# The compression's weight blocks take ring slots among the second group's last tiles

## The reference, cut to what matters

```python
def compress_blocks(t, pe, w1, w2):            # t: 256 tokens x 2 key heads x 128
    n_cmp = (s - CMP_BLOCK) // CMP_STRIDE + 1  # 15 blocks of 32 tokens, 16 apart
    idx = np.arange(n_cmp)[:, None] * CMP_STRIDE + np.arange(CMP_BLOCK)[None, :]
    blk = jnp.swapaxes(t[:, idx], 2, 3) + pe
    blk = blk.reshape(b, n_cmp, hk, CMP_BLOCK * d)
    return jax.nn.gelu(blk @ w1) @ w2          # w1: 4096 x 128
```

## Time and profile before

| | |
|---|---|
| median of 3 runs | 2350.07 us (2349.14 to 2352.84) |
| the profiled execution | 2346.51 us, span 2344.7 us |
| PE, DVE, ACT busy | 99%, 63%, 55% of the span |
| mean granted clock of PE | 0.996 |

### The profile page before, as it was taken

The page is one execution under the profiler, slowest core; times in us unless marked ns, Lnnn a source line. Parts: engine busy times, 40 slices in busy tenths (PEclk is TensorE's granted clock), DMA queues, the critical chain, the costliest instruction groups (busy, mean ns, idle before and its releaser), DMA issues.

```text
span 2344.7 us, 32539 instructions
## 1 busy us (share of the span) xinstructions
PE 2310.0 (99%) x12150; PEld 1951.4 (83%) x12150; DVE 1468.5 (63%) x2547; ACT 1299.5 (55%) x2374; POOL 18.3 (1%) x38
## 2 busy tenths in 40 slices
PE   8999999999999999999999999999999999999998
PEld 8877888788888888877888888888888888888886
DVE  5554565665665666876777666756566566665554
ACT  5644555665655545764556546546555555554444
POOL 1000000000000000000000000000000000000000
PEclk9999999999999999999999999999999999999999
DMA  7555565575445565656453326556666666665554
GB/s 230 171 163 151 171 206 189 153 189 171 127 145 195 154 182 174 188 168 177 141 170 111 107 81 234 198 187 177 191 189 189 189 189 189 189 207 190 192 189 165
DMA packets 239596, 409.07 MB, mean 174 GB/s; under 512 B 21504, under 2 KB 54576, under 8 KB 239056
## 3 DMA queue, kind: packets, MB, share of 16 engines
q1 hardware_dynamic: 235424, 393.07, 55.4%
q0 software_dynamic: 3152, 10.57, 1.2%
q10 hardware_dynamic: 864, 3.35, 0.4%
HBM read 400.65 MB, written 6.29 MB: 174 GB/s over the span
## 4 chain that ended last, share of the span: by engine, by line
PE 94%; DVE 3%; ACT 3%; issue 1%; DMA 0%; ACTq 0%; DVEq 0%
PE banks L390 52%; PE banks L354 17%; PE banks L356 8%; PE banks L384 5%; PE banks L841 1%; PE banks L681 1%; DVE weights_low L325 1%; ACT weights_high L322 1%; PE banks L2343 1%; PE banks L2354 1%; PE banks L1814 1%; PE banks L852 0%; PE banks L1207 0%; PE banks L859 0%; PE banks L861 0%
## 5 line engine op out<-in xcount | busy, mean ns | idle before, releaser
L325 DVE TENSOR_TENSOR weights_low<-weight_ring,weights_high 128x512 fp32r<-128x512 f32 x1464 | 997.4, 691 | 784.9 <-ACT weights_high L322 756.0
L322 ACT CAST weights_high<-weight_ring 128x512 fp32r<-128x512 f32 (+2 forms) x1476 | 904.5, 619 | 954.9 <-PE banks L390 607.5
L390 PE MATMUL banks<-weights_high,hidden_T 128*128 128x512 f32 x2976 | 853.9, 399 | 4.8 <-DVE weights_low L325 2.9
L390 PEld LDWEIGHTS banks<-weights_high,hidden_T 128*128 128x128 f32 x2976 | 550.3, 188 | 126.1 <-issue 9.9
L354 PE MATMUL banks<-hidden_T,weights_high 128*128 128x512 f32 x1728 | 543.3, 396 | 1.3 <-DVE weights_low L325 0.8
L390 PE MATMUL banks<-weights_low,hidden_T 128*128 128x512 f32 x1488 | 461.6, 391 | 0.0
L356 PEld LDWEIGHTS banks<-hidden_T,weights_low 128*128 128x128 f32 x1728 | 324.6, 188 | 76.7
L356 PE MATMUL banks<-hidden_T,weights_low 128*128 128x256 f32 x1728 | 339.5, 278 | 0.0
L390 PEld LDWEIGHTS banks<-weights_low,hidden_T 128*128 128x128 f32 x1488 | 280.1, 188 | 60.8
L354 PEld LDWEIGHTS banks<-hidden_T,weights_high 128*128 128x128 f32 x1728 | 263.1, 189 | 2.3 <-DVE weights_low L325 1.4
L390 PE MATMUL banks<-weights_high,ffn_high 128*128 128x512 f32 x344 | 106.3, 390 | 1.6 <-DVE weights_low L325 1.6
(11 more groups left out here) (426 smaller groups left out, 1801.3 us busy)
## 6 DMA issues: line engine op xcount, KB each, us to landing
weight_ring<-in_w_in SPq DMA_DIRECT2D x168, 512.0 KB, 3.6
weight_ring<-in_w_gla_in SPq DMA_DIRECT2D x96, 512.0 KB, 3.8
weight_ring<-in_w_gate SPq DMA_DIRECT2D x88, 512.0 KB, 3.6
weight_ring<-in_w_ffn_up SPq DMA_DIRECT2D x88, 512.0 KB, 3.7
weight_ring<-in_w_down SPq DMA_DIRECT2D x88, 512.0 KB, 3.8
weight_ring<-in_w_mla_in SPq DMA_DIRECT2D x48, 512.0 KB, 3.7
weight_ring<-in_w_gla_out SPq DMA_DIRECT2D x32, 512.0 KB, 4.5
weight_ring<-in_w_mla_out SPq DMA_DIRECT2D x32, 512.0 KB, 4.3
```

What stands on the lines that cost most here:

```text
L322: nc.scalar.copy(hi, raw).then_inc(high_ready, 1)
L325: nc.vector.tensor_tensor(lo, raw, hi.bitcast(F32), ALU.subtract).then_inc(low_ready, 1)
L390: last = pe.matmul(ps[:, b + t, 0:width], a[:, t * P:(t + 1) * P], w, start=(k == 0 and n_th == 0), stop=(k == kt - 1 and n_th == 2))
```

## The change

The product of the compression is gone as a stage. Its eight slots of weights become "visitors" among the uses of `prod_n`: one ahead of each of the tiles 64, 66, ... 78. SP loads them at that place, from weights that the host has laid out so that a partition's part is one run of 4 KB. PE multiplies a visitor with eight matmuls whose outputs go in turn to partitions 0, 32, 64 and 96 (32 stationary columns, two of them zero). The four partial sums are added later by a matmul with a constant matrix `fold_cmp` instead of a transpose.

All that ran beside the stage is laid into the slots of `prod_n` and `prod_z`. The turns of the compression's keys and values go from tile 55 to tile 53, the sums of squares to tiles 60 to 62, 73, 75, 77, 78 and 79, in three banks instead of four; the turns of the queries to z tiles 5, 6, 7 and 9 and those of the other keys to z tiles 25 and 26.

```diff
-                elif p == 55:
+                elif p == 53:
                     turn_nab.wait(pe)
                     prod_n.wait_chunk(pe, 2)
                     pe.wait_ge(n_rot, 1)
                     turn_n.tensor(pe, KC)
                     turn_n.tensor(pe, VC)
-                elif 64 <= p < 68:
+                elif 60 <= p < 63:
                     turn_n.wait(pe, VC)
-                    prepare_sum(pe, p - 64)
-                elif 76 <= p < 80:
+                    prepare_sum(pe, p - 60)
+                elif p in (73, 75, 77):
+                    prepare_sum(pe, 3 + (p - 73) // 2)
+                elif p in (78, 79):
                     prepare_sum(pe, p - 72)
+                if p >= CMP_AT and p % SLOT_K == 0:
+                    v = (p - CMP_AT) // SLOT_K
+                    if v % CMP_USES == 0:
+                        pe.wait_ge(blk_ready, v // CMP_USES + 1)
+                    compress(pe, v)
...
+        def compress(pe, v):
+            j, n = divmod(v, CMP_USES)
+            flat = prod_n.visit(pe, v)
+            for r in range(8):
+                rr = 8 * n + r
+                at = CMP_COLS * (rr % CMP_PARTS)
+                last = pe.matmul(ps[at:at + CMP_COLS, CMP_BANK, j * HD:(j + 1) * HD], n_blk[:, j, rr, :], flat[:, r * HD:(r + 1) * HD],
+                                 start=(rr < CMP_PARTS), stop=(rr >= CMP_BLOCK - CMP_PARTS), skip_group_check=True)
+            last.then_inc(native_used, 1)
...
+                            if m in self.visitors:
+                                sp.wait_ge(*freed[u - SLOTS])
+                                sp.dma_start(ring_flat[:, u % SLOTS, :], self.visitors[m]).then_inc(landed[u % SLOTS], 16)
+                                u += 1
+                            m += 1
...
+                elif p == 25:
+                    prod_n.wait_chunk(pe, 4)
+                    pe.wait_ge(n_rot, 3)
+                    pe.wait_ge(ab_cexp, 1)
+                    turn_n.tensor(pe, KS)
+                elif p == 26:
+                    pe.wait_ge(c_centred, 1)
+                    turn_n.tensor(pe, KW)
...
             Sc(act.activation(small_alog[:, :], small["alog"][:, :], ACT.Exp))
-            for g in range(4):
+            for g in range(3):
                 yield from pace.to(70 + g)
                 root_logarithm(g)
-            yield from pace.to(75)
-            Sc(act.activation(d_t0, d_t0, ACT.Ln, bias=1.0))
-            act.sem_inc(ab_exp, 1)
+            for g in range(3, 6):
+                yield from pace.to(68 + 2 * g)
+                root_logarithm(g)
...
+            prod_n.wait_evicted(v)
+            keys = itertools.chain(rotate_keys(0), rotate_keys(1))
+            for _ in range(4):
+                yield from pace.to(pace.slot + 1)
+                next(keys)
             yield from pace.to(20)
...
             v.sem_inc(c_centred, 1)
+            yield from pace.to(22)
+            next(keys)
+            yield from pace.to(23)
+            for _ in keys:
+                pass
+            v.sem_inc(n_rot, 1)
...
-        L2_BANK = (4, 5, 6, 7, 4, 5, 6, 7)
+        L2_BANK = (4, 5, 6, 4, 5, 6, 4, 5)
...
-            if g >= 4:
-                pe.wait_ge(l2_log, g - 3)
+            if g >= 3:
+                pe.wait_ge(l2_log, g - 2)
```

More of the change, by code:

```diff
@@ L219, in program, with __init__ @@
         class Product:
-            def __init__(self, chunks, rounds=1, native=False):
-                self.chunks, self.rounds, self.native = chunks, rounds, native
+            def __init__(self, chunks, rounds=1, visitors={}):
+                self.chunks, self.rounds, self.visitors = chunks, rounds, visitors
                 self.use0, self.chunk0, self.tile0 = planned["use"], planned["chunk"], planned["tile"]
-                self.uses = sum(c[1] // slot_tiles(c) for c in chunks)
-                self.tiles = 0 if native else sum(c[1] for c in chunks)
-                self.native0, self.nchunk0 = planned["native"], planned["native_chunk"]
+                own = sum(c[1] // slot_tiles(c) for c in chunks)
+                self.at = [m + sum(v <= m for v in visitors) for m in range(own)]
+                self.visits = [self.at[m] - 1 for m in sorted(visitors)]
+                self.uses = own + len(visitors)
+                self.tiles = sum(c[1] for c in chunks)
+                self.native0 = planned["native"]
                 planned["use"] += self.uses * rounds
@@ L301, in place_of, with visit @@
                     uses += k // slot_tiles(self.chunks[n])
+                uses = self.at[uses] if uses < len(self.at) else self.uses
                 return self.use0 + uses, self.tile0 + sum(c[1] for c in self.chunks[:n]) + k
+            def visit(self, pe, v):
+                u = self.visits[v]
+                pe.wait_ge(landed[(self.use0 + u) % SLOTS], self.landing[u])
+                return ring_flat[:, (self.use0 + u) % SLOTS, :]
             def split(self, eng, i, n, k):
@@ L1796, in program @@
         prod_nab = Product([stacked_columns(A["w_nab"], NAB)])
[L1797 removed]
+        CMP_AT, CMP_USES, CMP_BANK = 64, CMP_BLOCK // 8, 7
+        prod_n = Product([(A["w_in2"], KD, n * W, 0, W, hidden, False) for n in range(5)],
+                         visitors={CMP_AT // SLOT_K + CMP_USES * j + n: A["cmp_w1"][j][:, n * 8 * HD:(n + 1) * 8 * HD]
+                                   for j in range(2) for n in range(CMP_USES)})
         nabT = extra[0:2 * NAB, 2560:2560 + S]
@@ L2029, in z_side_scalar @@
             pace = Pace()
-            for n, g in enumerate((KS, KW)):
-                yield from pace.to(2 + n)
-                turn_n.scalar(g)
+            for g in (6, 7):
+                root_logarithm(g)
+                yield from pace.to(g - 5)
+            for g in range(4):
+                yield from pace.to(2 + g)
+                inverse_root(g)
+            yield from pace.to(6)
+            turn_n.scalar(Q0)
             yield from pace.to(7)
@@ L2036, in z_side_scalar @@
             act.sem_inc(c_tanh, 1)
-            yield from pace.to(11)
-            prepare_exps()
+            turn_n.scalar(Q0 + 1)
+            yield from pace.to(8)
+            turn_n.scalar(Q0 + 2)
+            yield from pace.to(9)
+            inverse_root(4)
+            yield from pace.to(10)
+            turn_n.scalar(Q0 + 3)
+            for g, slot in ((5, 12), (6, 14), (7, 15)):
+                yield from pace.to(slot)
+                inverse_root(g)
+                if g == 5:
+                    yield from pace.to(13)
+                    prepare_exps()
             yield from pace.to(22)
@@ L2042, in z_side_scalar @@
             act.sem_inc(c_exped, 1)
+            for n, g in enumerate((KS, KW)):
+                yield from pace.to(26 + n)
+                turn_n.scalar(g)
         def nsa_scalar(one):
@@ L2144, in copy_tokens @@
+            yield from pace.to(66)
+            next(value_blocks)
+            yield from pace.to(67)
+            for _ in value_blocks:
+                pass
+            yield from pace.run(query_steps)
+            V(v.memset(c_g, 0.0))
+            query_steps = rotate_queries(1)
+            yield from pace.run(query_steps, 2)
+            v.sem_inc(n_rot, 1)
+            yield from pace.to(79)
+            for j in range(2):
+                copy_tokens(j)
         def copy_tokens(j):
-            c = prod_cmp.chunk0 + j
@@ L2153, in z_side_vector @@
             pace = Pace()
-            for g in range(4):
-                yield from pace.to(g)
-                prepare_head(g)
+            yield from pace.to(3)
+            prepare_decays()
             yield from pace.to(4)
-            prepare_decays()
+            prepare_head(0)
             yield from pace.to(5)
@@ L2165, in z_side_vector @@
             v.sem_inc(c_lin, 1)
-            for g in range(4, 6):
-                yield from pace.to(2 + g)
+            for g in range(1, 3):
+                yield from pace.to(5 + g)
                 prepare_head(g)
@@ L2176, in z_side_vector @@
             v.sem_inc(c_act, 1)
+            for g in range(3, 5):
+                yield from pace.to(8 + g)
+                prepare_head(g)
             yield from pace.to(13)
@@ L2215, in z_side_vector @@
             v.sem_inc(c_probs, 1)
+            for g in range(5, DN_H):
+                yield from pace.to(21 + g)
+                prepare_head(g)
+            v.sem_inc(l2_done, 1)
             yield from pace.to(30)
@@ L3270, in _ @@
             prod_nab.run(v, after=prod_n)
-            prod_n.run(v, side=n_side_vector())
-            cmp_vector()
+            prod_n.run(v, after=prod_z, side=n_side_vector())
             prod_z.run(v, after=prod_gates, side=z_side_vector())
```

216 lines of the change are left out of this document (91 added, 125 removed).

## The result

| | before | changed |
|---|---|---|
| median of 17 runs each | 2349.67 us (2347.52 to 2353.9) | 2352.54 us (2350.0 to 2357.97) |
| ratio | | 1.0014, interval 1.0007 to 1.002 |
| the profiled execution | 2346.51 us, span 2344.7 | 2357.24 us, span 2355.4 |

What follows compares the result with a forecast made beforehand. PE's own instruction list plus its few waits was taken as the bound; -18.0 us for the removed stage against turns, visits, waits and clock summed to +1.4, a 2351.5 us median. Its own range was 2349 to 2355, the full range 2346 to 2359.

Steps and rivals of the forecast that it cites:

- turns and token matmuls: Five turns moved from the stage to between tiles, +2.4 us; two token transposes become two-pass matmuls, +0.2 us.
- visits: Eight visits of 16 passes among `prod_n` tiles, half overlapped, at 1.15 us each: +9.2 us, bounds 5.6 and 16.0.
- wait 1: Ahead of `prod_n` tile 53, PE waits for DVE's last rotation before the keys' turns: +2.65 us.
- wait 2: At `prod_n` tile 73, PE waits for the first logarithm, behind tile 74's split and its late weight load: +2.65 us.
- wait 3: At z tile 25, PE's turn waits for the last rotation, behind DVE's split of z tile 27: +2.1 us.
- short waits, others: Short waits of PE on splits in `prod_n`, absorbed by the pause at tile 53: -0.4 us.
- clock: Granted clock falls after one in three of the new pauses, 1.7 us each: +0.6 us, bounds 0 and 5.
- rival B: In the visits, full packing with four groups at once, 0.7 us a visit: -0.7 us, 2349.4 us; chance 0.13.
- At nothing: ACT and DVE work from the removed stage fits between splits, free; splits late up to 1 us a visit at 0.7.
- Rival A: In the visits, no overlap between groups, 2.0 us a visit: +7.4 us, 2357.5 us; chance 0.20.
- C: At tile 73 and z tile 25, waits mostly absent, no clock loss: -2 to -4.9 us, 2345 to 2348; chance 0.15.
- D: The clock falls in all three new pauses, three times 1.7 us: +5.9 us, 2356 us; chance 0.07.

## Why the prediction was right, and where it was not

| term | forecast | measured in the stretch |
|---|---|---|
| stage removed | -18.0 | -18.1 |
| turns and token matmuls | +2.6 | +2.4 |
| visits | +9.2 | +6.7 |
| wait 1 | +2.65 | +2.7 |
| wait 2 | +2.65 | +3.3 |
| wait 3 | +2.1 | +2.3 |
| short waits, others | -0.4 | +0.3 |
| sum without the clock | +0.8 | -0.4 |
| clock | +0.6 | +3.3 here; +2.8 as the mean loss of all executions |

The time came out right because the sum's terms were the right ones, and because two mis-sized ones have opposite signs: the visits were 2.5 too dear and the clock 2.7 too cheap. That these cancel is luck.

*The visits* failed in their mechanism: "the two passes of one matmul share a group and can't overlap" was what put 0.87 between the bounds of 0.44 and 1.75. The rows and the runs with one and two groups show that the passes start in fours, so rival B had the packing right, at the lower bound of 0.44. It also had what follows from it, a longer wait 2 and 1 us of late splits. The change of shape cost 0.39 instead of 0.25 (the 0.25 came from a tile with a 30-row matmul, another shape), so a visit stood at 0.84 rather than B's 0.7. My reading of the rule on program order was too strong: that matmuls start in order did not keep four from starting together.

*Waits 1 and 3* were right in place, releaser and size; to take wait 3 away returns 1.5 of its 2.3 in the tiles. *Wait 2* was right in its chain, and the run with ACT's list shortened shows the landing as its cause. It was 0.7 longer. The load was not issued with the visitor's (1034.51) but 1.0 later (1035.52), as DVE freed its slot, and took 4.8, so it landed 0.5 later than forecast; the chain behind the landing took 0.4 more, and PE came 0.2 later.

*At nothing* was nearly right: splits were late by 0.95 in three tiles (68, 72, 79), where I allowed up to 1 a visit.

*The clock* was the largest error. I priced one pause in three at 1.7. The mean loss rose by 2.8, with an error of 0.7. The longest pause, wait 2, was followed by a fall in all four profiles that have it, the other two in one of eight; this alone is 1.7 where I had 0.6. The other 1.7 in the table is the longer fall behind z tile 17. That place had none, a short or a long one in profiles of kernels that are alike there, so it can't be put down to the change. With any single wait removed the mean loss stayed at 13.5 to 13.7, with all three it fell to 10.3. Why it did not fall when wait 2 went is open; its error is as large as what one would look for. The pauses are not its only cause either: the kernel with one group has none of the three and lost 13.0, and the packed stage 13.4.

*Rival A* is out (2.0 a visit is the one-group kernel's figure). C is out: both waits are there in full. The version without the waits reached its -8 with full packing, but because the waiters were moved, not because loads land sooner or DVE is in time. C's lower end was mis-added: with both waits gone it gives -4.0, not -4.9, and its time ends at 2346; the rest of the forecast doesn't hang on it. The mean loss of 2.8 lies between the forecast's 0.6 and the 5.1 of D; why it is that much is shown in part only.

## What to carry to other kernels

Work that is taken out of a stage and laid among tiles pays in waits at the places where it lands: list each new wait with its releaser and move the waiter by as many tiles as the wait is long before judging the idea. Here moving three waiters by two tiles each turned +2.9 us into -8.0. And small float32 matmuls in distinct groups of 32 columns were worth the full factor of the groups here, less a fixed 0.35 to 0.39 for going in and out; I would count them so at first. What such a packing saves arrives only as far as the next engine lets it: late splits took 1.6 back here, and in the stage, where the first 64 passes alone were 5.2 shorter, ACT let 2.6 through.

## What I had not expected of the hardware

- Float32 matmuls with 32 stationary columns, two passes each, start in fours when their outputs go to four groups: 64 passes in 1.95 us against 7.17 in one group.
- A change of the stationary shape costs (0.35 to 0.39 for 32 columns), but small matmuls with 128 stationary columns and 16 moving ones go in and out at next to no price: four groups of eight passes took 0.92 each, which is 0.115 a pass, one group of 32 took 3.6.
- Behind a pause of PE of 3.3 to 3.6 us the granted clock fell in four profiles of four, behind pauses of 1.9 to 2.6 in one of eight. The four are all at the same place, so length and place aren't told apart.
- At 50 us, where the program is the same, the granted clock was 0.53 in one execution and 1.00 in another. The difference of two single profiles' spans (10.7) was almost four times that of the medians (2.9).
